# The gated blocks' stores and fetches of the six feed-forward stages are issued by GpSimd instead of SyncE

## What is computed

```python
def swiglu(h, w_gate_up, w_down):
    gu = h @ w_gate_up
    g, u = jnp.split(gu, 2, axis=-1)
    return (jax.nn.silu(g) * u) @ w_down
```

## Time and profile before

| | |
|---|---|
| median of 3 runs | 1775.55 us (1773.31 to 1779.73) |
| the profiled execution, its own time | 1775.69 us |
| its span | 1774.0 us |
| TensorE matmul busy | 1759.9 us, 99% |
| VectorE busy | 1196.6 us, 67% |
| ScalarE busy | 907.7 us, 51% |
| GpSimd busy | 93.0 us, 5% |
| DMA engines, queue of SyncE | 65.7% of 16 engines |
| DMA engines, queue of GpSimd | 1.4% |
| stores / fetches | 132 / 132, 3.1 / 4.8 us to landing (median) |

### The profile page before, as it was taken

One profiled execution on the slowest core, in us unless ns is written; L12 is line 12 of the kernel. 1 busy time (PEld: TensorE's weight loads), 2 busy tenths in 40 slices (PEclk: granted clock), 3 DMA queues, 4 the chain that ended last, 5 costly groups with the idle time before them and its releaser, 6 DMA issues.

```text
span 1774.0 us, 22288 instructions
## 1 busy us (share of the span) xinstructions
PE 1759.9 (99%) x8335; PEld 1473.2 (83%) x8335; DVE 1196.6 (67%) x1592; ACT 907.7 (51%) x1382; POOL 93.0 (5%) x209
## 2 busy tenths in 40 slices
PE   8999999999999999999999999999999999999998
PEld 7888888888888888888888888888888888888887
DVE  8868766876756676666676766567566668676655
ACT  6655444666544554445455544455444546454443
POOL 4001000200000010001000100001000100010000
PEclk9999999999999999999999999999999999999999
DMA  8337776643787777776686577767877668557773
GB/s 265 119 119 218 226 223 200 195 140 96 226 245 222 219 220 237 246 224 214 195 255 204 172 217 235 228 214 222 244 248 223 213 200 260 193 170 245 228 220 122
DMA packets 320923, 370.83 MB, mean 209 GB/s; under 512 B 82896, under 2 KB 253936, under 8 KB 320560
## 3 DMA queue, kind: packets, MB, share of 16 engines
q1 hardware_dynamic: 318336, 361.65, 65.7%
q0 software_dynamic: 2176, 7.75, 1.4%
q10 hardware_dynamic: 304, 0.01, 0.0%
HBM read 346.81 MB, written 22.54 MB: 208 GB/s over the span
## 4 chain that ended last, share of the span: by engine, by line
PE 94%; DMA 3%; DVE 2%; issue 0%; ACT 0%; SPq 0%; DVEq 0%; POOLq 0%; POOL 0%; ACTq 0%
PE Dp L1928 18%; PE Dp L1930 17%; PE Dp L1929 17%; PE Tp L1930 6%; PE Tp L1928 6%; PE Tp L1929 6%; PE Gp L1930 6%; PE Gp L1928 6%; PE Gp L1929 6%; DMA held_piece<-inner 1%; DMA Z<-held 1%; PE Gp L2104 1%; PE Tp L2095 1%; DVE wlo L1234 1%; PE Dp L2128 1%; DMA held<-Z 1%
## 5 line engine op out<-in xcount | busy, mean ns | idle before, releaser
L1234 DVE TENSOR_TENSOR wlo<-raw,whi 128x1024 fp32r<-128x1024 f32 (+1 forms) x608 | 711.5, 1207 | 321.1 <-ACT whi L769 320.6
L769 ACT ACTIVATE whi<-raw 128x1024 fp32r<-128x1024 f32 (+1 forms) x608 | 607.5, 1045 | 450.8 <-PE Dp L1930 255.1
L1928 PE MATMUL Dp<-whi,a_hi 128*128 128x512 f32 (+2 forms) x768 | 292.8, 381 | 4.1 <-DVE a_lo L1299 2.7
L1930 PE MATMUL Dp<-whi,a_lo 128*128 128x512 f32 (+2 forms) x768 | 287.9, 375 | 0.0
L1929 PE MATMUL Dp<-wlo,a_hi 128*128 128x512 f32 (+2 forms) x768 | 287.5, 374 | 0.0
L1928 PE MATMUL Dp<-whi,b_hi 128*128 128x512 f32 (+1 forms) x492 | 194.4, 395 | 0.7 <-DVE wlo L1234 0.7
L1930 PE MATMUL Dp<-whi,b_lo 128*128 128x512 f32 (+1 forms) x492 | 191.5, 389 | 0.0
L1929 PE MATMUL Dp<-wlo,b_hi 128*128 128x512 f32 (+1 forms) x492 | 191.2, 389 | 0.0
L1928 PE MATMUL Gp<-whi,a_hi 128*128 128x512 f32 x480 | 186.7, 389 | 0.0
L1930 PE MATMUL Gp<-whi,a_lo 128*128 128x512 f32 x480 | 186.7, 389 | 0.0
L1929 PE MATMUL Gp<-wlo,a_hi 128*128 128x512 f32 x480 | 186.7, 389 | 0.0
(11 more groups left out here) (262 smaller groups left out, 2056.3 us busy)
## 6 DMA issues: line engine op xcount, KB each, us to landing
raw<-in_ffn_w_gate_up SPq DMA_DIRECT2D x176, 512.0 KB, 5.0
raw<-in_w_in SPq DMA_DIRECT2D x132, 512.0 KB, 4.8
raw<-in_ffn_w_down SPq DMA_DIRECT2D x88, 512.0 KB, 4.5
raw<-in_w_gate SPq DMA_DIRECT2D x44, 512.0 KB, 4.2
raw<-in_w_up SPq DMA_DIRECT2D x44, 512.0 KB, 5.3
raw<-in_w_down SPq DMA_DIRECT2D x44, 512.0 KB, 4.6
held<-Z SPq DMA_DIRECT2D x132, 128.0 KB, 3.1
Z<-held SPq DMA_DIRECT2D x132, 128.0 KB, 4.8
```

Of the source, the lines that this page charges most:

```text
L769: return nc.scalar.activation(whi[g % W][0:rows, c0:c0 + n], raw[g % R][0:rows, c0:c0 + n], ACT.Copy).then_inc(hi_done, 1)
L1234: return V.tensor_tensor(wlo[g % W][0:rows, c0:c0 + n], raw[g % R][0:rows, c0:c0 + n], whi[g % W][0:rows, c0:c0 + n].bitcast(F32), ALU.sub ...
L1928: mm(o, hi, wh, start=start, stop=False, skip_group_check=True)
L1930: return mm(o, lo, wh, start=False, stop=stop, skip_group_check=True)
```

## The change

SyncE keeps only the weight loads and the convolution mixer's pieces. GpSimd's program gets the same `store` and `fetch`, with the same waits, and calls them from a new function `gated(F, j)` between a stage's `x_rstd` and `y_rstd`, for j = 0 to 10. The order within it is fixed: the store of tile 0's *next* chunk, the store of tile 1's chunk, the fetch of tile 0's next chunk, the fetch of tile 1's chunk. The three gain loads of the first FFN of a second-block layer lose their wait and stand ahead of j = 5, 7 and 9. Transfers, buffers and semaphores are the same.

```diff
@@ SyncE
-            def store(t, F, j):
-                n = NJ * F + j
-                sp.wait_ge(blocked[t], n + 1)
-                if n:
-                    sp.wait_ge(fetched[t], 16 * n)
-                sp.dma_start(held[t], blocks(t)).then_inc(stored[t], 16)
-            def fetch(t, F, j):
-                sp.wait_ge(stored[t], 16 * (NJ * F + j + 1))
-                if NJ * F + j:
-                    sp.wait_ge(flo[t], NJ * F + j)
-                sp.dma_start(Z[...], held[t]...).then_inc(fetched[t], 16)
@@ behind(g): the loops over F and j go
@@ GpSimd
+            def store(t, F, j):
+                n = NJ * F + j
+                pool.wait_ge(blocked[t], n + 1)
+                if n:
+                    pool.wait_ge(fetched[t], 16 * n)
+                pool.dma_start(held[t], blocks(t)).then_inc(stored[t], 16)
+            def fetch(t, F, j):
+                pool.wait_ge(stored[t], 16 * (NJ * F + j + 1))
+                if NJ * F + j:
+                    pool.wait_ge(flo[t], NJ * F + j)
+                pool.dma_start(Z[...], held[t]...).then_inc(fetched[t], 16)
+            def gated(F, j):
+                if j == 0:
+                    store(0, F, 0)
+                    fetch(0, F, 0)
+                if j + 1 < NJ:
+                    store(0, F, j + 1)
+                store(1, F, j)
+                if j + 1 < NJ:
+                    fetch(0, F, j + 1)
+                fetch(1, F, j)
@@ each FFN stage, between x_rstd and y_rstd
+                for j in range(NJ):
+                    gated(f_1(l), j)
@@ first FFN of a second-block layer
-                for j, n in enumerate(("ffn1_post_2", "mix_post_2", "ffn2_post_2")):
-                    pool.wait_ge(fm[0], NJ * f_21(l) + 2 * j + 5)
-                    pool.dma_start(gp[j][:, :], ...)
+                for j in range(NJ):
+                    if j in (5, 7, 9):
+                        pool.dma_start(gp[(j - 5) // 2][:, :], ...)
+                    gated(f_21(l), j)
```

More of the change, by code:

```diff
@@ L452, in _ @@
             x_half(0, 0)
-            def store(t, F, j):
-                n = NJ * F + j
-                sp.wait_ge(blocked[t], n + 1)
-                if n:
-                    sp.wait_ge(fetched[t], 16 * n)
-                sp.dma_start(held[t], blocks(t)).then_inc(stored[t], 16)
-            def fetch(t, F, j):
-                sp.wait_ge(stored[t], 16 * (NJ * F + j + 1))
-                if NJ * F + j:
-                    sp.wait_ge(flo[t], NJ * F + j)
-                sp.dma_start(Z[:, MOVED + FC * t:MOVED + FC * t + FC].rearrange("p (q n) -> p q n", q=4),
-                             held[t].rearrange("(q c) (b n) -> (c b) q n", q=4, b=4)).then_inc(fetched[t], 16)
             def store_piece(l, i):
@@ L494, in behind @@
                         store_piece(l, i)
[L496 to L510, removed]
             def put(g, parts):
@@ L611, in _ @@
             behind(LAST + 1)
-            behind(LAST + 2)
             ov = out.rearrange("a (t p) d -> p (a t) d", p=P)
@@ L712, in augment @@
                 pool.tensor_copy(zf[t][:, 1, :, HD + 1:HD + 2], cumk[:, t, :].unsqueeze(2)).then_inc(aug[t], 1)
+            def store(t, F, j):
[8 more added lines that the diff above has]
+                    pool.wait_ge(flo[t], NJ * F + j)
+                pool.dma_start(Z[:, MOVED + FC * t:MOVED + FC * t + FC].rearrange("p (q n) -> p q n", q=4),
+                               held[t].rearrange("(q c) (b n) -> (c b) q n", q=4, b=4)).then_inc(fetched[t], 16)
+            def gated(F, j):
[8 more added lines that the diff above has]
+                fetch(1, F, j)
             for l in range(LAYERS):
@@ L743, in _ @@
                     x_rstd(t, s)
-                for j, n in enumerate(("ffn1_post_2", "mix_post_2", "ffn2_post_2")):
-                    pool.wait_ge(fm[0], NJ * f_21(l) + 2 * j + 5)
-                    pool.dma_start(gp[j][:, :], A[n][l].partition_broadcast(P)).then_inc(gains_in[1], 16)
+                for j in range(NJ):
+                    if j in (5, 7, 9):
+                        n = ("ffn1_post_2", "mix_post_2", "ffn2_post_2")[(j - 5) // 2]
+                        pool.dma_start(gp[(j - 5) // 2][:, :], A[n][l].partition_broadcast(P)).then_inc(gains_in[1], 16)
+                    gated(f_21(l), j)
                 for t in range(2):
@@ L758, in _ @@
                     x_rstd(t, s)
+                for j in range(NJ):
+                    gated(f_22(l), j)
                 for t in range(2):
```

## The result

The changed kernel takes 1786.95 us (median of four runs, 1785.32 to 1788.07), the kernel before in the same session 1774.91 (four runs, 1773.31 to 1779.73). The ratio is 1.0068, with an interval of 1.0056 to 1.0080: 12 us slower. The forecast was 1774.8 and no change. The spans differ by 12.3 us (1786.3 against 1774.0 us), so the two traces can be compared end to end.

What follows compares the result with a forecast made beforehand. TensorE, busy 1759.9 of 1774.0 us, was taken as the bound, with transfers staying hidden (chance 0.70). The profiled 1775.69 us less 0.9 for one stall gave 1774.8, other parts costed at nothing; range 1772.5 to 1792.

Steps and rivals of the forecast that it cites:

- rival 1: Loop in steady chunks: each chunk slips above L of 10.9 us; at 12 us, 1806 us in total; chance 0.22.
- the steady chunk: Middle of a stage: ScalarE waits about 2.5 us for tile 1's fetch in nearly every chunk, TensorE for nothing.
- L: Steady chunk, from tile 0's block ready to tile 1's fetch landed: 10.1 us, bounds 4.5 and 16.2.
- 100 us and more in all: Sign of being right: ScalarE's total wait for fetches, some 2.5 us about 8 times a stage.
- the 2.6 us of cover: Steady chunk: lateness of ScalarE's rounding, past 1119.7, that TensorE does not feel until 1122.3.
- port lock: GpSimd's DMA issues each wait out a VectorE instruction of 1.2 us: 17 us a stage, 1877 us; chance 0.05.
- The end of a stage: `y_rstd` behind the last fetch, issued at 1186.94: no cost at 0.8 us of issue, 2 us at 2.1.
- `y_rstd` waits for GpSimd: Sign of being wrong, at a stage's end: `y_rstd` waits for GpSimd rather than for ScalarE's squares.
- SyncE loses 264 issues and their waits: SyncE's queue: weight loads wait for splits of units, not for issues; costed at nothing either way.
- The start of a stage: Fetches issued 2 to 3 us earlier, ahead of the next load; the one stall goes, a gain of 0.9 us.

Runs made afterwards that it cites:

- e9_late3: e6_both plus five one-column powers on GpSimd between tile 0's and tile 1's fetch in chunks 2 to 8; 1919.57 us, ratio 1.0816.
- e1_tail: Changed kernel with the last store and fetch of tile 1 in each stage back on SyncE at their old place; 1779.61 us, ratio 1.0029.
- e5_hold: Changed kernel with SyncE waiting at each stage's end until GpSimd's last transfers have landed; 1781.35 us, ratio 1.0046.
- e2_iota: Changed kernel with GpSimd's two iotas of the first FFN stage put behind the first store; 1782.58 us, ratio 1.0046.
- e6_both: Changed kernel with the edits of e1_tail and e2_iota together; 1774.68 us, ratio 1.0004.
- e4_order: Changed kernel with tile 1's store and fetch ahead of tile 0's in chunks 2 to 8; 1786.79 us, ratio 1.0066.

## Why the prediction was right, and where it was wrong

The forecast was no change, and the kernel is 12 us slower. That 1786.95 lies in the stated range, up to 1792, is luck: its upper part was kept for rival 1, which did not happen. Three things that the prediction cost at nothing or as a gain failed: the end of a stage, the loss of SyncE's waits, and the start of the first stage.

**Right: the steady chunk.** The sum was L = 10.1 us and the median is 10.1; the fetch's issue, of which no row was at hand, was taken at 0.8 between 0.54 and 2.1 and is 0.76. That the sum fits to a tenth is in part luck. The store was taken at 4.0 and the fetch at 5.2, and the medians of these chunks are 3.7 and 4.9; the way from the block to the store's issue was taken at 0.1 and is 0.3, and that from the store's landing to the issue of tile 1's fetch was taken at 0.8 and is 1.0. These errors make up for each other. ScalarE waits 179 us ("100 us and more in all"), TensorE for nothing, also in the six chunks where L was past the 10.9 of rival 1, up to 12.3: a late chunk uses up some of the 2.6 us of cover, and the next one gives it back. The loop of rival 1 is real (e9_late3); it simply was not reached. Its own items add up to 5.65 us and not to "about 5.5", so its threshold was 10.7 and the forecast lay 0.6 below it.

**Right: no port lock.** 132 fetch issues take 747 to 779 ns, 132 stores 545 to 659, beside a VectorE that is busy two thirds of the span. By the rule of the Trainium skill (SBUF — State Buffer, Who interferes with whom) that the prediction weighed, the trace agrees: the spread is at most 0.11 us, and no issue waited out one of VectorE's instructions of 1.2 us.

**Wrong: "The end of a stage", costed at nothing.** The prediction took the last fetch as issued at 1186.94, where the kernel before had it, and asked only for its longer issue. But the last fetch stands at the end of a string, in which tile 1's last store waits for the fetch before it to land, and the last fetch for that store, and the whole string moved. That is 7.3 us (e1_tail). The prediction's own sign of it came true: `y_rstd` waits for GpSimd (621.43, right behind the issue of 620.61) and not for ScalarE's squares. The mistake was to take a start time from the trace of before for an instruction whose releasers the change had touched.

**Wrong: "SyncE loses 264 issues and their waits ... I cost it at nothing", and that, of the cover, a load which goes out earlier "only lengthens it".** SyncE's waits did work: they kept the loads behind the transfers that end a stage. e5_hold adds waits and nothing else, and 5.6 us return by the medians; by the matmul starts 4.0 us return at the ends. The trace of before had it: there the pair at the end of the second stage lands in 2.4 and 2.7 us, near the lowest of the earlier trace rows, against a median of 4.8. The Trainium skill (DMA: Bandwidth & Descriptors, Issuing engines are not separate DMA queues) says that DMAs started by different engines run on the same DMA engines and interleave. By that rule, the trace agrees: the pair takes 2.7 and 2.8 us with no load in flight (e5_hold), and 5.4 and 5.1 behind two loads of another queue.

**Wrong: "The start of a stage", which was to gain 0.9 us.** The gain came: the stall of the earlier trace rows is gone; measured against TensorE's work, the fetch that landed late there is issued 1.6 us earlier and lands 2.3 us earlier. But "ahead of the next load" was taken for all six starts. In the five others the first store goes out 1.4 us later than before, behind `x_rstd`, lands in 2.1 to 2.3 us, and costs nothing. In the first GpSimd comes from 2.2 us of its own work, issues its store only 0.2 us ahead of the load, and the late landing is handed on to the fetch, the next store and the next fetch. The prediction counted GpSimd's work over a stage (30 us of 180) and not what stood right ahead of the first store. That is 4.4 us (e2_iota).

So the total of 12 us is 7.3 and 4.4, each found again by undoing it, and both at once bring the time of before back (e6_both). At the ends the trace of e5_hold shows two parts: the pair, late behind loads, which the waits bring back, and the last fetch, which stays late (5.3 to 5.9 us in the second to fifth stages, 2.2 to 2.3 before) because the first of the held loads goes out 0.3 to 0.5 us ahead of it. Not settled is how much of the second part is GpSimd's: its longer issue of the pair (1.51 us against 0.92), `y_rstd` behind the last fetch, and that SyncE's held loads may cost something by themselves; no run parts them. That the store of the first stage is slow for the load's sake fits all nine traces with the store on GpSimd (4.2 to 4.9 us at 0.18 us ahead, 2.7 to 3.2 at 0.78), but each time the iotas had moved too, and no run moved the load alone.

## What to carry to other kernels

A wait on a queue is also a brake on everything behind it: before you free a queue from its waits, look which transfers land fast because of them. When transfers move to another engine, rebuild the first and the last of each stage as strings of waits, link by link, and read what the new engine does right ahead of the first; the steady middle, where most of the DMAs are, can be free while a dozen at the edges cost the whole. A small transfer that goes out 0.2 us ahead of a large one on another queue should be counted as beside it.

## What the runs showed of the hardware that was not expected

**GpSimd's DMAs make fewer packets.** The page counts 244892 packets where the kernel before had 320923, and 15313 under 512 B against 82896, for the same transfers; the fetch of 256-byte runs lands no sooner for it (4.9 us, 4.8 before).

**The granted clock after a stall.** In the changed kernel TensorE stands from 168.6 to 171.8 us, and soon after its matmuls start 0.43 us apart and not 0.23, eight of them:

```profile
173.29 0.63 PE L1929 MATMUL Gp<-whi,a_hi 128*128 128x512 f32 x1
173.72 0.63 PE L1930 MATMUL Gp<-wlo,a_hi 128*128 128x512 f32 x1
```

The granted clock of 171.8 to 176 us is 0.67 of full speed, a mean of stretches at 2.4 and at 1.2 GHz; eight times 0.2 us is 1.6 of the 4.4 us. In e1_tail it stays at 1.00, and in e5_hold it falls again. The lines are of the changed kernel, e1_tail and e5_hold:

```profile
171.80:176.00 4.20, 4.20 (x13) 3.33 (x14) 4.17 (x8) 0.97 (x2) 1.52 (x2) 0.67 0.62 190
```

```profile
171.80:176.00 4.20, 3.33 (x15) 2.79 (x16) 4.20 (x6) 1.82 (x2) 1.99 (x3) 1.00 0.50 140
```

```profile
171.80:176.00 4.20, 4.20 (x14) 3.32 (x13) 4.17 (x9) 0.40 (x1) 1.24 (x2) 0.65 0.65 208
```

The length of the stall alone does not decide it. From the last matmul's start before it to the first behind it are 3.25 us in the changed kernel, 3.06 in e4_order and 2.75 in e5_hold, and in all three the clock falls; in e1_tail they are 3.04, and it does not.

In e9_late3, where TensorE stands for 99.6 of 1911.3 us, the granted clock of the run is 0.977 and its busy time is 1811.7 us, 48 more than the changed kernel's. Yet the loop's sum accounts for the stages without them; I read that as slow stretches that lie where TensorE would have stood anyway, which no run tested.
